# Two-layer hybrid block on one core: how each expert's token rows are gathered on TensorE

## What is computed

```
g_sel = argmax(softmax(xf @ w_group))                    # 4 groups
top_p, top_i = top_k(softmax(e_logits of that group), 2) # 2 of 8 experts
rows = xpad[row_tok]                                     # tokens of each expert
h = silu(rows @ w_gate[e]) * (rows @ w_up[e])            # 1024 -> 512
yb = h @ w_down[e]                                       # 512 -> 1024
out = segment_sum(yb * row_w, row_tok)                   # back to the tokens
```

## Time and profile before

| | |
|---|---|
| median of 3 runs | 2253.1 us (2251.59 to 2255.76) |
| span of the profiled execution | 2257.6 us |
| TensorE busy | 2090.0 us, 93% |
| VectorE busy | 745.3 us, 33% |
| ScalarE busy | 364.6 us, 16% |
| transfers | 565.33 MB, mean 250 GB/s |
| mean granted clock of TensorE | 0.895 |

### The profile page before, as it was taken

The page is one execution under the profiler, slowest core; times in us unless marked ns, Lnnn a source line. Parts: engine busy times, 40 slices in busy tenths (PEclk is TensorE's granted clock), DMA queues, the critical chain, the costliest instruction groups (busy, mean ns, idle before and its releaser), DMA issues.

```text
span 2257.6 us, 32970 instructions
## 1 busy us (share of the span) xinstructions
PE 2090.0 (93%) x13605; PEld 1401.4 (62%) x13605; DVE 745.3 (33%) x2250; ACT 364.6 (16%) x968; POOL 86.5 (4%) x92
## 2 busy tenths in 40 slices
PE   8999999998888798999998888897999999799998
PEld 7687576765655444576666565444688544458863
DVE  4354242221212315522222222467222115733211
ACT  2222110100000113210000000114221001322100
POOL 0112100000000100000000000000001000000110
PEclk9999977988888897777878888997999999889999
DMA  9333459999999952469999999941344344214420
GB/s 338 130 113 120 146 204 402 424 423 425 425 425 423 401 207 82 147 263 425 426 424 424 424 425 424 340 150 38 120 154 150 126 149 152 73 62 172 149 93 19
DMA packets 112382, 565.33 MB, mean 250 GB/s; under 512 B 12456, under 2 KB 15726, under 8 KB 79470
## 3 DMA queue, kind: packets, MB, share of 16 engines
q1 hardware_dynamic: 112238, 563.21, 63.1%
HBM read 562.14 MB, written 1.05 MB: 249 GB/s over the span
## 4 chain that ended last, share of the span: by engine, by line
PE 86%; DVE 5%; DMA 4%; issue 4%; ACT 1%; SPq 0%; DVEq 0%; ACTq 0%
PE ps L2434 14%; PE ps L669 11%; PE ps L1633 11%; PE ps L650 10%; PE ps L295 9%; PE ps L708 7%; PE ps L1200 5%; DMA ring<-in_moe_w_up_dram 4%; PE ps L761 3%; PE ps L1306 3%; PE ps L1210 2%; PE ps L690 2%; PE ps L1976 1%; PE ps L1719 1%; DVE tiny L1806 1%
## 5 line engine op out<-in xcount | busy, mean ns | idle before, releaser
L2434 PE MATMUL ps<-arena,ring 128*128 128x256 f32 (+1 forms) x1536 | 305.5, 362 | 0.0
L2434 PEld LDWEIGHTS ps<-arena,ring 128*128 128x128 f32 x1536 | 271.9, 190 | 33.9 <-issue 1.0
L650 PEld LDWEIGHTS ps<-arena 128*128 128x128 f32 x2048 | 247.2, 201 | 27.6 <-issue 26.6
L1633 PE MATMUL ps<-ring,arena 128*128 128x512 f32 (+1 forms) x576 | 251.1, 595 | 3.8 <-DVE arena L420 3.8
L650 PE MATMUL ps<-arena 128*128 128x32 f32 x2048 | 254.0, 285 | 0.0
L669 PE MATMUL ps<-ring,arena 128*32 128x256 f32 x2816 | 189.1, 424 | 46.0 <-issue 35.8
L295 PE MATMUL ps<-ring,arena 128*128 128x512 f32 x480 | 211.9, 602 | 0.8 <-ACT arena L2277 0.8
L1633 PEld LDWEIGHTS ps<-ring,arena 128*128 128x128 f32 x576 | 109.9, 193 | 136.4 <-issue 136.1
L669 PEld LDWEIGHTS ps<-ring,arena 128*32 128x32 f32 x2816 | 112.8, 123 | 122.8 <-issue 86.9
L295 PEld LDWEIGHTS ps<-ring,arena 128*128 128x128 f32 x480 | 92.5, 194 | 115.3 <-issue 113.6
L2494 DVE SCALAR_TENSOR_TENSOR arena<-ps,pcol,arena 128x255 f32<-128x255 f32 (+1 forms) x176 | 84.8, 482 | 210.8 <-ACT arena L2467 207.7
(11 more groups left out here) (306 smaller groups left out, 1974.6 us busy)
## 6 DMA issues: line engine op xcount, KB each, us to landing
ring<-in_moe_w_gate_dram SPq DMA_DIRECT2D x44, 2048.0 KB, 29.5
ring<-in_moe_w_up_dram SPq DMA_DIRECT2D x44, 2048.0 KB, 33.9
ring<-in_moe_w_down_dram SPq DMA_DIRECT2D x44, 2048.0 KB, 30.4
ring<-in_w_up_dram SPq DMA_DIRECT2D x22, 2048.0 KB, 8.1
arena<-in_moe_w_gate_dram SPq DMA_DIRECT2D x20, 2048.0 KB, 29.2
arena<-in_moe_w_up_dram SPq DMA_DIRECT2D x20, 2048.0 KB, 33.7
arena<-in_moe_w_down_dram SPq DMA_DIRECT2D x20, 2048.0 KB, 31.1
ring<-in_ssm_w_in_dram SPq DMA_DIRECT2D x12, 2048.0 KB, 9.8
```

The costliest lines, as they stand in the source:

```text
L650: mm = nc.tensor.matmul(ps[:, 4, k * CAP:(k + 1) * CAP], normed[:, tt, k, :], slots[:, b, tt, :], start=(tt == 0), stop=(tt == TT - 1))
L1633: mm = nc.tensor.matmul(ps[:, bank + n % 4, 0:n_cols], xT[:, k, tt * P:(tt + 1) * P], w[:, k, :], start=(k == 0), stop=(k == KD - 1))
L2434: mm = nc.tensor.matmul(ps[:, n % 4, lo:hi], w[:, k, k4 * P:(k4 + 1) * P], xT_mlp[:, k, lo:hi], start=(k == 0), stop=(k == KD - 1))
```

## The change

The slots become the stationary operand and the normed tokens the moving one: for each of two token tiles and four column groups one product, 32 slots against 256 features (feature tiles 2j and 2j+1) into partitions 32j to 32j+31 of bank 4. That gives slots x features. ScalarE copies the 128x256 result to `chosen_rows` (`step_pick_copy`), and PE turns its two halves back into bank 4 (`step_pick_turn`). `step_xg` then runs over the two halves apart, and since half c holds the feature tiles c, c+2, c+4 and c+6, `step_gateup` reads `xg` in another order.

```diff
--- before.py
+++ after.py
@@ -603,7 +603,7 @@
         xT_second = area(20112, KD, SEQ)
         n_second = area(8080, TT, D)
         turned_gb = (tiny[:, 276:284], tiny[:, 284:292])
-        STEP_SEMS = ("slots", "picked", "xg_scaled", "xg", "gateup", "silu", "hidden", "turned", "hT", "down", "rows_act",
+        STEP_SEMS = ("slots", "picked", "pick_copied", "pick_turned", "xg_scaled", "xg", "gateup", "silu", "hidden", "turned", "hT", "down", "rows_act",
                      "rows_dve", "back", "back_turned", "back_copied")
         MAIN = {n: sem("moe_" + n) for n in ("combined",) + STEP_SEMS}
         OVER = [{n: sem(f"over{layer}_" + n) for n in ("loaded", "shifted", "free") + STEP_SEMS} for layer in range(2)]
@@ -621,6 +621,7 @@
             slots = area(2336, 2, TT, CAP)
             xg = area(3072, 2, KD * CAP)
             sg = area(3584, 2, 256)
+            chosen_rows = area(6976, 2, 256)
             hid = area(4096, 2, 256)
             hT = area(4608, 2, 2, 2 * CAP)
             back = area(4864, TT, P)
@@ -645,28 +646,47 @@
 
             def step_pick(pe, s, v, b):
                 pe.wait_ge(s["slots"].sem, v(s["slots"]))
-                for k in range(KD):
-                    for tt in range(TT):
-                        mm = nc.tensor.matmul(ps[:, 4, k * CAP:(k + 1) * CAP], normed[:, tt, k, :],
-                                              slots[:, b, tt, :], start=(tt == 0), stop=(tt == TT - 1))
+                for tt in range(TT):
+                    for j in range(4):
+                        mm = nc.tensor.matmul(ps[j * CAP:(j + 1) * CAP, 4, 0:256], slots[:, b, tt, :],
+                                              normed[:, tt, 2 * j:2 * j + 2, :].rearrange("p a b -> p (a b)"),
+                                              start=(tt == 0), stop=(tt == TT - 1))
                 mm.then_inc(s["picked"].sem, 1)
 
+            def step_pick_copy(act, s, v, prev, b):
+                act.wait_ge(s["picked"].sem, v(s["picked"]))
+                if prev:
+                    act.wait_ge(s["pick_turned"].sem, prev(s["pick_turned"]))
+                nc.scalar.activation(chosen_rows[:, b, :], ps[:, 4, 0:256], ACT.Copy).then_inc(s["pick_copied"].sem, 1)
+
+            def step_pick_turn(pe, s, v, b):
+                pe.wait_ge(s["pick_copied"].sem, v(s["pick_copied"]))
+                for c in range(2):
+                    mm = nc.tensor.transpose(ps[:, 4, c * P:(c + 1) * P], chosen_rows[:, b, c * P:(c + 1) * P], ident)
+                mm.then_inc(s["pick_turned"].sem, 1)
+
             def step_xg(dve, s, v, prev, b):
-                dve.wait_ge(s["picked"].sem, v(s["picked"]))
+                dve.wait_ge(s["pick_turned"].sem, v(s["pick_turned"]))
                 if prev:
                     dve.wait_ge(s["gateup"].sem, prev(s["gateup"]))
-                x = xg[:, b, :].rearrange("p (k c) -> p k c", k=KD)
-                nc.vector.tensor_tensor(x, ps[:, 4, 0:KD * CAP].rearrange("p (k c) -> p k c", k=KD),
-                                        bcast(g_mix, CAP), ALU.mult).then_inc(s["xg_scaled"].sem, 1)
+                for c in range(2):
+                    x = xg[:, b, c * P:(c + 1) * P].rearrange("p (j c) -> p j c", j=4)
+                    ins = nc.vector.tensor_tensor(x, ps[:, 4, c * P:(c + 1) * P].rearrange("p (j c) -> p j c", j=4),
+                                                  bcast(g_mix[:, c:KD:2], CAP), ALU.mult)
+                ins.then_inc(s["xg_scaled"].sem, 1)
                 dve.wait_ge(s["xg_scaled"].sem, v(s["xg_scaled"]))
-                nc.vector.tensor_tensor(x, x, bcast(b_mix, CAP), ALU.add).then_inc(s["xg"].sem, 1)
+                for c in range(2):
+                    x = xg[:, b, c * P:(c + 1) * P].rearrange("p (j c) -> p j c", j=4)
+                    ins = nc.vector.tensor_tensor(x, x, bcast(b_mix[:, c:KD:2], CAP), ALU.add)
+                ins.then_inc(s["xg"].sem, 1)
 
             def step_gateup(pe, s, v, b, wg, wu):
                 pe.wait_ge(s["xg"].sem, v(s["xg"]))
                 for k in range(KD):
                     for j in range(4):
                         w = (wg, wu)[j // 2]
-                        mm = nc.tensor.matmul(ps[j * CAP:(j + 1) * CAP, 5, 0:256], xg[:, b, k * CAP:(k + 1) * CAP],
+                        mm = nc.tensor.matmul(ps[j * CAP:(j + 1) * CAP, 5, 0:256],
+                                              xg[:, b, (k % 2 * 4 + k // 2) * CAP:(k % 2 * 4 + k // 2 + 1) * CAP],
                                               w[:, k, (j % 2) * 256:(j % 2 + 1) * 256],
                                               start=(k == 0), stop=(k == KD - 1))
                 mm.then_inc(s["gateup"].sem, 1)
@@ -868,12 +888,15 @@
                     if i == 2:
                         pe.wait_ge(m["back_copied"].sem, m["back_copied"].at(q + 1))
                     step_turn(pe, m, v, b)
+                    if not is_last(q, i):
+                        step_pick_turn(pe, m, next_views(q, i)[1], 1 - b)
                     arrived(2)
                     step_down(pe, m, v, before, b, w[2])
                     if i == 1:
                         step_back_turn(pe, m, m["back"].at(q + 1), 4)
 
                 step_pick(pe, m, lambda s: s.at(1), 0)
+                step_pick_turn(pe, m, lambda s: s.at(1), 0)
                 for i in range(4):
                     expert(0, i, i % 3, i // 3)
                 with pe.Fori(0, 2) as r:
@@ -888,6 +911,7 @@
                             v = over_view(z)
                             pe.wait_ge(o["loaded"].sem, 48 * (z + 1))
                             step_pick(pe, o, v, 1)
+                            step_pick_turn(pe, o, v, 1)
                             step_gateup(pe, o, v, 1, wf[0][0], wf[0][1])
                             step_turn(pe, o, v, 1)
                             step_down(pe, o, v, None, 1, wf[0][2])
@@ -905,9 +929,14 @@
             def experts_act(act):
                 head.act_exps(act)
 
+                step_pick_copy(act, m, lambda s: s.at(1), None, 0)
+
                 def expert(q, i):
                     e, v, prev, before = views(q, i)
                     step_silu(act, m, v, prev, i % 2)
+                    if not is_last(q, i):
+                        e1, v1, prev1, _ = next_views(q, i)
+                        step_pick_copy(act, m, v1, prev1, 1 - i % 2)
                     read = None if first_quad(q) else q
                     if i == 2:
                         step_back_copy(act, m, m["back_turned"].at(q + 1), read, 4)
@@ -925,6 +954,7 @@
                         with act.Fori(0, NE) as e:
                             z = (r - 1) * NE + e
                             v = over_view(z)
+                            step_pick_copy(act, o, v, None, 1)
                             step_silu(act, o, v, None, 1)
                             step_rows_act(act, o, v, None, 0, y_over)
                             step_back_copy(act, o, z + 1, None, 1, backT_over)
```

## The result

| | before | changed |
|---|---|---|
| median, first comparison | 2252.3 us (2251.01 to 2255.76, 5 runs) | 2241.89 us (2236.15 to 2241.98, 5 runs) |
| ratio | | 0.995, 95% interval 0.9935 to 0.9965 |
| median, second comparison (last experiments) | 2252.07 us (16 runs) | 2241.28 us (11 runs) |
| ratio | | 0.9956, 0.994 to 0.9972 |
| span of the first profile | 2257.6 us | 2237.9 us |

What follows compares the result with a forecast made beforehand. Weight loads, 14.8 us per expert, were taken to bound both expert stages. 12.5 us gained from starts and holes less 3.4 lost to clock gave -9.1 us on the profiled run, carried to a 2244.0 us median, range 2237 to 2253.

Steps and rivals of the forecast that it cites:

- first pick to first products (P to G0): Start of each expert stage: expert 0's gate and up products start 3.5 us earlier in layer 0, 3.7 in layer 1.
- clock in those products: Expert 0's gate and up products: no clock gain in the sum, only up to 3 us less within the range.
- stream of loads (hole): Expert 3's down load, issued after the queue ran dry: earlier issue closes the gap, 3.6 and 1.7 us gained.
- tail (G31 to N): Expert 31's gate and up products start colder, 5.35 us each: 1.7 us lost per layer, 3.4 together.
- a warmer first product: Start of the stages: first products at a better clock, 3 us less, used for the range's low end.
- Nothing in mid stage: Middle of both stages: weights set 14.8 us per expert, so a shorter pick buys only idle time on PE.
- Rival C: Steady part: clock stays at half over whole experts, PE becomes the bound at 16.6 us each; about 2345 us, chance 0.03.
- rival D: Pick: the four column groups don't overlap, 16 records take 6.1 us in all; 2260 us, chance 0.03.
- Rival A: Tail of both stages goes cold altogether: up to 18.4 us given back, 2259 us, 2250 in the middle; chance 0.15.
- Rival B: Weight queue: late buffer releases empty it and eat the lead, only the colder tail shows; 2253 to 2256 us, chance 0.08.

Runs made afterwards that it cites:

- the two in which the crowded branch ran: Kernel before and changed kernel, each loading only a quarter of the down weights of experts 3 to 31 in both layers: 11146.41 and 10147.33 us.
- lighter loads: Kernel before and changed kernel, each loading a quarter of the down weights of experts 3 to 31, in layer 1 alone: 2216.42 and 2142.56 us.

## Why the prediction was right

The time (2241.89 against 2244.0 forecast, in a range of 2237 to 2253) and the direction came out, and the pairs of profiles let each term be compared (both layers together, means of two profiles for each kernel):

| term | forecast | measured |
|---|---|---|
| first pick to first products (P to G0) | -7.2 | -7.9 (16.0 to 8.1) |
| clock in those products | 0, up to 3 us as a bound | -3.4 (12.4 to 9.0) |
| stream of loads (hole) | -5.3 | -5.7 (873.2 to 867.5) |
| tail (G31 to N) | +3.4 | +5.5 (38.2 to 43.8) |
| sum | -9.1 | -11.4 (by the medians -10.4 and -10.8) |

- **Start.** The pick was longer than priced, 1.94 us where I took 1.64; the copy, the turning and the passes came out shorter than I priced them: the two transposes ran in 0.44 us, and two 128x128 passes together took 0.49 us, not 0.58. VectorE had finished the gate weights before the turned pick was there, so PE and ScalarE set the start, not VectorE.
- **First products at full clock.** This is the term that I mis-sized: I left the products at the clock they had and kept "a warmer first product" for the range. It is less firm than the table has it. In ten stages with the old first pick, in the profiles of nearly all versions, they took 5.03 to 6.58 us, 5.97 on the mean; in the ten with the new one and no idle products 3.66 to 6.58, 5.27 on the mean. The change's own two profiles lie on the good side of that; by the means the term is -1.4. (Left out of both means are the version without the awake-keeping product and the two in which the crowded branch ran.) Idle products bring it to 3.66 us in both layers, as shown above; what decides the clock without them, no experiment isolates.
- **Hole.** 5.3 forecast, 5.7 measured. The reasoning held in the main: with the new gather for experts 1 to 31 the hole is closed, with it for 2 to 31 it stays. But the down load came 6.1 us behind the gate load and not 9 or 10. Of the 7.3 us less in layer 0 the shorter pick gives 3.4, the term I had; the other 3.8 are the products behind it, which now ran at full clock (see the last section). And the 5.7 agree with 5.3 partly by luck, since the same distance also shrank by 4.2 us over both layers where the hole stayed (experts 2 to 31). The throughput in the first 90 us from expert 3's gate load is the more direct measure: 400 and 407 GB/s before, 417 and 416 now, 5.5 us.
- **Nothing in mid stage.** 14.74 us per expert, share 1.01, before and after. PE's busy time fell by 210 us where I had said some 170. Rival C (PE becomes the bound) is out; so is rival D, as 16 records take 1.05 us.
- **Tail.** The direction was right and the size low: 2.3 and 2.4 us for G31 where I took 1.7, as the wait grew to 5.7 and 6.0 us, and 0.8 us more up to the next stage. By the Trainium skill's page TensorE: Matmul & The Clock Gate, section Why this matters for your kernels, gaps between bursts should be avoided. The rows here agree (5.92 us behind a gap of 5.70), and the version with idle products shows the remedy. The length of the gap alone doesn't decide: with experts 2 to 31 new, expert 31 ran in 3.66 us behind a gap of 3.48. Rival A's worst form did not come: turn, down and combine ran at full clock.
- **Rival B** (the lead is lost on the way) is out: what was gained at G0 is still there at G31.

The two mis-sized terms, the first products (-3.4) and the tail (+2.1, of it 1.3 by the clock), partly cancelled. That the forecast was closer than its parts is luck; which spans set the time, and which didn't, was not.

## What to carry to other kernels

Where a stream of loads sets the pace, an engine's saved time counts only ahead of the first load that waits for it, and behind the last; price those two ends, and leave the middle at nothing, however large its share of the page. Look at which short stretches hold back the next transfer: two gathers of 64 gave 8.3 us, and sixty of the others nothing that could be told. Time saved on TensorE in front of a wait can come back as a colder array behind it; products without a use, placed in that wait, are a cheap remedy when the product behind them is on the path.

## What the runs showed that I had not expected

- **A busy PE at half clock.** PE stood at half clock although it was busy throughout: in the kernel before, the window from 330 to 335 us shows PE busy 5.00 of 5.00 us at a granted clock of 0.50, just behind the pick for expert 1. With the new pick the same place, 316 to 332 us, is at 1.00 with PE busy 14.72 of 16:

```profile
330.00:335.00 5.00, 5.00 (x24) 4.96 (x24) 0.77 (x3) 0.00 (x0) 0.00 (x0) 0.50 1.00 423
```

```profile
316.00:332.00 16.00, 14.72 (x214) 10.38 (x210) 7.50 (x29) 3.01 (x8) 0.00 (x0) 1.00 0.90 368
```

  Being busy did not keep the array at full clock here. The partial versions separate what did it. With the new gather for expert 0 alone, the products behind the old pick of expert 1 (L480, then turn) ran at half clock:

```profile
327.86 3.65 PE L480 MATMUL ps<-arena 128*128 128x64 f32 x16
331.44 1.11 PE L735 MATMUL ps<-cst,arena 64*128 64x64 f32 x4
```

  With experts 1 to 31 new, the same products stood behind the new pick, after first products just as cold (6.51 us against 6.47), and ran at full clock:

```profile
326.51 1.98 PE L480 MATMUL ps<-arena 128*128 128x64 f32 x16
328.42 0.68 PE L735 MATMUL ps<-cst,arena 64*128 64x64 f32 x4
```

  It holds in every profile: turn of expert 0 took 1.11 us in all 12 stages with the old pick for expert 1 and 0.68 in all 16 with the new one. So it is the old pick ahead of them (32 records of 32 moving columns, 4.55 us, against 16 records in 1.05), not idle time; by which mechanism, no run here shows. It is seen at the end of the stages too: expert 30's down products, behind the old pick, took 3.34, 3.25 and 3.58 us in three of the four profiled stages of before (1.93 in the fourth), and 1.93 or 1.94 in all four of the changed kernel. The pick at full clock that my prediction set against rival A was therefore no sign that the clock would stay. All this fits the larger gain under lighter loads, where the clock of before is 0.86 with PE 95% busy, and that of the change 0.93 with PE 80% busy.
- **Scatter ahead of the stage.** The same code up to the first pick took 304.6 to 311.9 us. Spans of single profiles can't show a change of 10 us in this kernel; distances inside the stage can.
